# Adding the experts' rows to the residual stream by an accumulating scatter, in a one-core diffusion block with a mixture of experts

## The reference

```python
h2 = modulate(rmsnorm(x, g_norm2[i]), sh2, sc2)          # x * rstd * g * (1 + scale) + shift
moe = hierarchical_moe(h2, ...)                          # per token: best of 4 groups, best 2 of its 8 experts
#   gate  = top_w / sum(top_w) * p(group)                # one gate for each of a token's two experts
#   y     = (silu(x @ w_gate[e]) * (x @ w_up[e])) @ w_down[e]
#   moe   = zeros(n, d).at[slot_tok].add(y * slot_gate)  # each token gets two gated rows
x = x + gt2 * moe
return rmsnorm(x, g_final)
```

## Time and profile before

| | |
|---|---|
| runs, us | 1279.66, 1282.55, 1283.43; median 1282.55 |
| profiled execution, us | 1280.05, with a span of 1278.2 from first to last instruction |
| TensorE | busy 1225.1 us (96% of the span) |
| VectorE | busy 956.4 us (75%) |
| ScalarE | busy 679.8 us (53%) |
| GpSimd | busy 262.6 us (21%) |
| mean granted TensorE clock | 0.983 of full |
| moved by DMA | 344.34 MB, mean 269 GB/s |

### The profile page before, as it was taken

How to read it: one execution, slowest core, us unless ns; L and a number is a source line. 1 busy time by engine, 2 the same in 40 slices (tenths; PEclk the granted TensorE clock), 3 DMA queues, 4 the chain that set the end, 5 groups by cost and what they waited for, 6 DMA issues and landing times. The chain is left out here.

```text
span 1278.2 us, 18789 instructions
## 1 busy us (share of the span) xinstructions
PE 1225.1 (96%) x7362; PEld 1020.9 (80%) x7362; DVE 956.4 (75%) x1128; ACT 679.8 (53%) x806; POOL 262.6 (21%) x210
## 2 busy tenths in 40 slices
PE   5899999999999999999979999999999999999986
PEld 1799888888788888888768888888888888888863
DVE  2756554332678888666669999999999999999956
ACT  3832212111556666332247777777777777777722
POOL 0000000001100010000110634525355173611111
PEclk9899999999999999999899999999999999999988
DMA  9658844435576774610469999999999999999937
GB/s 380 244 187 294 285 148 155 159 113 171 201 227 143 186 176 109 216 58 34 143 232 370 369 399 384 383 389 374 387 380 382 385 369 398 382 387 374 379 121 303
DMA packets 95659, 344.34 MB, mean 269 GB/s; under 512 B 18459, under 2 KB 46803, under 8 KB 67923
## 3 DMA queue, kind: packets, MB, share of 16 engines
q1 hardware_dynamic: 74659, 311.89, 67.0%
q10 hardware_dynamic: 11696, 14.44, 3.9%
q0 software_dynamic: 9216, 16.80, 3.5%
HBM read 314.23 MB, written 39.34 MB: 277 GB/s over the span
## 5 line engine op out<-in xcount | busy, mean ns | idle before, releaser
L2150 DVE TENSOR_TENSOR w_low<-raw,w_high 128x2048 fp32r<-128x2048 f32 x130 | 296.1, 2298 | 6.2 <-ACT w_high L2096 6.1
L2096 ACT ACTIVATE w_high<-raw 128x2048 fp32r<-128x2048 f32 x130 | 244.5, 1908 | 8.5 <-PEq L1386 8.5
L2150 DVE TENSOR_TENSOR w_low<-arena,w_high 128x2048 fp32r<-128x2048 f32 x62 | 142.6, 2303 | 27.1 <-ACT w_high L2096 27.1
L2051 POOL DMA_INDIRECT y_rows<-arena,row x32 | 68.3, 2136 | 315.6 <-DVE arena L2172 314.1
L2096 ACT ACTIVATE w_high<-arena 128x2048 fp32r<-128x2048 f32 x62 | 118.2, 1907 | 0.0
L1996 PE MATMUL p_g<-w_high,x_high 128*128 128x512 f32 x252 | 102.3, 406 | 1.9 <-DVE w_low L2150 1.1
L1996 PE MATMUL p_u<-w_high,x_high 128*128 128x512 f32 x256 | 102.8, 402 | 0.0
L1996 PE MATMUL p_a<-tokens_high,half_high 128*128 128x512 f32 (+1 forms) x272 | 101.9, 374 | 0.2 <-DVE half_low L699 0.2
L1997 PE MATMUL p_a<-tokens_low,half_high 128*128 128x512 f32 (+1 forms) x272 | 101.0, 371 | 0.0
L1998 PE MATMUL p_a<-tokens_high,half_low 128*128 128x512 f32 (+1 forms) x272 | 100.9, 371 | 0.0
L1998 PE MATMUL p_u<-w_high,x_low 128*128 128x512 f32 x256 | 100.0, 391 | 0.0
(11 more groups left out here) (388 smaller groups left out, 2848.7 us busy)
## 6 DMA issues: line engine op xcount, KB each, us to landing
raw<-in_w_gate SPq DMA_DIRECT2D x64, 1024.0 KB, 8.4
raw<-in_w_up SPq DMA_DIRECT2D x64, 1024.0 KB, 8.5
arena<-in_w_down SPq DMA_DIRECT2D x62, 1024.0 KB, 8.5
raw<-in_w_ada SPq DMA_DIRECT2D x24, 1024.0 KB, 7.4
x<-qk_rows SPq DMA_DIRECT2D x6, 1664.0 KB, 8.7
raw<-in_w_chunks SPq DMA_DIRECT2D x9, 1024.0 KB, 5.6
qk_rows<-x SPq DMA_DIRECT2D x18, 512.0 KB, 2.6
mod<-x ACTq DMA_DIRECT2D x48, 128.0 KB, 3.3
```

The costliest lines, as they stand in the source:

```text
L2051: pool.indirect_dma_start(a.y_rows, bass.IndirectOffsetOnAxis(ap=s.row[:, n:n + 1], axis=0), x.y[b], None, bounds_check=2 * N - 1, oob_is_ ...
L2096: act.activation(x.high[i % SPLITS][:], x.raw[b][:, :], ACT.Copy).then_inc(high_ok, 1)
L2150: dve.tensor_tensor(x.low[i % SPLITS][:], x.raw[home(n, j)][:, :], x.high[i % SPLITS][:], ALU.subtract).then_inc(low_ok, 1)
```

## The change

1. **The stream is stored.** SP stores each tile of `s.x1` to a new DRAM array `stream_rows` (1024 rows) after `residual(n)`, between the weight loads that it issues there; `x_stored` counts them.
2. **The scatter accumulates.** It goes to `stream_rows` by `token`, with `compute_op=ALU.add`. Since a token's two rows now go to one place, each scatter first waits until the one before has landed. `y_rows` and `row` are gone.
3. **Gates by slot.** The gates are split into three bfloat16 parts, multiplied into the one-hot choice by VectorE at the head of the experts' block, and TensorE lists them by slot in 16 matmuls before the first expert. `move_y` multiplies by `slot_gates` in the same instruction. The table for tiles beyond 128 tokens gets gates in the same way: three GpSimd instructions and 16 matmuls more before expert 27.
4. **Only the sums are read back.** `finish` loads 512 KB for each tile into `s.x1`, squares, and scales. TensorE and GpSimd have no part in it; each group's Newton step is on VectorE.
5. **The last tile is modulated by VectorE**: one multiplication before `move_x(7)`, one fused multiply-add after its Newton step; the store waits for `scaled_last` 2.
6. `list_rows` is two instructions ahead of the gather, not four. `match` lives in the expert buffer `y5[0]`, so it waits for the store of tile 6.

```diff
-NORMS = [(0, 1), (1, 1), (2, 2), (4, 2), (6, 2)]
+NORMS = [(0, 1), (1, 2), (3, 2), (5, 2), (7, 1)]
@@ mix_and_route, SP
                 load_chunk(sp, a, s.raw[0], s.loaded[0], 0, 0)
+                def store_stream(i):
+                    sp.wait_ge(added, 2 * (i + 1))
+                    sp.dma_start(a.stream_rows[i * P:(i + 1) * P, :], s.x1[:, i, :]).then_inc(s.x_stored, 16)
+                for i in range(NT - 2):
+                    store_stream(i)
                 sp.wait_ge(split_low, 3 * NT - 2)
                 load_chunk(sp, a, s.raw[RING - 1], s.loaded[RING - 1], 0, RING - 1)
+                store_stream(NT - 2)
...
-                sp.wait_ge(scaled_last, 4)
+                sp.wait_ge(scaled_last, 1)
                 load_chunk(sp, a, s.raw[1], s.loaded[1], 0, 1)
                 sp.wait_ge(logits, NT + 1)
                 load_chunk(sp, a, s.raw[2], s.loaded[2], 0, 2)
+                store_stream(NT - 1)
@@ mix_and_route, GpSimd and ScalarE
-                pool.tensor_tensor(last[:], last[:], scale2, ALU.mult).then_inc(scaled_last, 1)
-                pool.tensor_tensor(last[:], last[:], shift2, ALU.add).then_inc(scaled_last, 1)
...
-                act.activation(xrow[(NT - 1) % 2][:], s.x1[:, NT - 1, :], ACT.Copy, scale=rstd[:, 2, NT - 1:NT])
@@ mix_and_route, VectorE
                     if n == NT - 1:
+                        dve.wait_ge(scaled_last, 1)
+                        stt(last[:], last[:], rstd[:, 2, one], shift2, ALU.mult, ALU.add).then_inc(scaled_last, 1)
+                def scale_last():
+                    dve.wait_ge(added, 2 * NT)
+                    dve.wait_ge(h_out[(NT - 1) % 2], 16 * (NT // 2 - 1))
+                    tt(xrow[(NT - 1) % 2][:], s.x1[:, NT - 1, :], scale2, ALU.mult).then_inc(scaled_last, 1)
...
+                dve.wait_ge(h_out[0], 16 * NT // 2)
...
+                for d in range(2):
+                    step(dve.tensor_copy(s.gate_parts[:, d, :], flat_gates))
+                    step(tt(flat_gates, flat_gates, s.gate_parts[:, d, :], ALU.subtract))
+                step(dve.tensor_copy(s.gate_parts[:, 2, :], flat_gates))
@@ main_experts, GpSimd
                 pool.wait_ge(y_ok, n + 1)
-                pool.indirect_dma_start(a.y_rows, ...s.row..., x.y[b], None, bounds_check=2 * N - 1).then_inc(scattered[b], 16)
+                pool.wait_ge(s.x_stored, 16 * NT) if n == 0 else pool.wait_ge(scattered, 16 * n)
+                pool.indirect_dma_start(a.stream_rows, ...s.token..., x.y[n % 2], None, bounds_check=N - 1,
+                                        compute_op=ALU.add).then_inc(scattered, 16)
@@ main_experts, VectorE
-                    dve.wait_ge(scattered[n % 2], 16 * (n // 2))
+                    dve.wait_ge(scattered, 16 * (n - 1))
-                dve.tensor_tensor(halves(x.y[n % 2]), p_y, halves(x.gate2[:]), ALU.mult)
+                dve.scalar_tensor_tensor(halves(x.y[n % 2]), p_y, s.slot_gates[:, n:n + 1], halves(x.gate2[:]), ALU.mult, ALU.mult)
+            def code_gates():                                   # called first in the block
+                for d in range(3):
+                    dve.tensor_tensor(x.gate_code[:, :, d, :], one_e, s.gate_parts[:, d, :]..., ALU.mult).then_inc(q.gate_coded, 1)
@@ main_experts, TensorE
+            def list_gates():                                   # called between stay_awake and turn_x(0)
+                pe.wait_ge(q.gate_coded, 3)
+                for u in range(2 * NT):
+                    listed = pe.matmul(x.p_list[:, 0:3 * NE], s.match[:, u, :], x.gate_code[:, u]...)
@@ finish
+        for i in range(NT):
+            sp.dma_start(s.x1[:, i, :], a.stream_rows[i * P:(i + 1) * P, :]).then_inc(x_in[i], 16)
...
+            for i in range(t0, t0 + n):
+                act.wait_ge(x_in[i], 16)
+                act.activation(junk[i], s.x1[:, i, :], ACT.Square, accum_out=ss[:, i:i + 1]).then_inc(rooted, 1)
+            act.activation(root[:, part], ss[:, part], ACT.Sqrt, ...).then_inc(rooted, 1)
...
+            c.step(dve.reciprocal(rstd[:, part], root[:, part]))
+            newton(dve, c, rstd[:, part], ss[:, part], tmp[:, part], D, n=1)
             for i in range(t0, t0 + n):
                 dve.scalar_tensor_tensor(x1, x1, rstd[:, i:i + 1], gains[:], ALU.mult, ALU.mult).then_inc(scaled, 1)
```

More of the change, by code:

```diff
@@ L1588, in norm_x @@
                     if n == NT - 1:
-                        dve.sem_inc(scaled_last, 1)
+                        last = xrow[n % 2]
+                        dve.wait_ge(scaled_last, 1)
+                        stt(last[:], last[:], rstd[:, 2, one], shift2, ALU.mult, ALU.add).then_inc(scaled_last, 1)
                         return
@@ L1686, in _ @@
                 dve.wait_ge(placed, 2)
-                list_rows(dve, c, p_t[0][:, 0:2 * NE], rowf[:], wrap[:], s.token[:], s.row[:], listed_ok)
+                list_rows(dve, c, p_t[0][:, 0:2 * NE], wrap[:], s.token[:], listed_ok)
                 step(dve.tensor_copy(total, p_r[:, NT * NE:(NT + 1) * NE]))
@@ L1808, in gather, with list_rows @@
                             bounds_check=N - 1, oob_is_err=False).then_inc(s.gathered[n % 2], 16)
-def list_rows(dve, c, digits, rowf, wrap, token, row, listed=None):
+def list_rows(dve, c, digits, wrap, token, listed=None):
     n = token.shape[1]
[L1815 to L1818, removed]
+    c.step(dve.tensor_scalar(wrap, digits[:, n:2 * n], float(N), None, ALU.add))
+    tokens = dve.scalar_tensor_tensor(token, digits[:, 0:n], -float(P), wrap, ALU.mult, ALU.add)
     if listed is None:
@@ L1849 @@
 class OverTables:
-    STEPS = 80
+    STEPS = 83
     def __init__(self, s, x):
@@ L2047, in scatter @@
             def scatter(n):
-                b = n % 2
                 pool.wait_ge(y_ok, n + 1)
-                pool.indirect_dma_start(a.y_rows, bass.IndirectOffsetOnAxis(ap=s.row[:, n:n + 1], axis=0), x.y[b], None,
-                                        bounds_check=2 * N - 1, oob_is_err=False).then_inc(scattered[b], 16)
+                if n == 0:
+                    pool.wait_ge(s.x_stored, 16 * NT)
+                else:
+                    pool.wait_ge(scattered, 16 * n)
+                pool.indirect_dma_start(a.stream_rows, bass.IndirectOffsetOnAxis(ap=s.token[:, n:n + 1], axis=0), x.y[n % 2], None,
+                                        bounds_check=N - 1, oob_is_err=False, compute_op=ALU.add).then_inc(scattered, 16)
             steps = Counter(pool, over_ready)
@@ L2074, in _ @@
                 if n == 16:
-                    over.blocks(pool, steps)
+                    over.blocks(pool, steps, s)
                 if n == 19:
@@ L2081, in _ @@
             count = spare.count(pool)
-            for b in range(2):
-                pool.wait_ge(scattered[b], 16 * (NE // 2))
+            pool.wait_ge(scattered, 16 * NE)
             spare.gpsimd(pool, count)
@@ L2168, in move_y, with add_parts @@
                 if n >= 2:
-                    dve.wait_ge(scattered[n % 2], 16 * (n // 2))
+                    dve.wait_ge(scattered, 16 * (n - 1))
                 halves = lambda y: y.rearrange("p (c n) -> p c n", c=2)
                 p_y = p_last if n == NE - 1 else x.p_y[:]
-                dve.tensor_tensor(halves(x.y[n % 2]), p_y, halves(x.gate2[:]), ALU.mult).then_inc(y_ok, 1)
+                dve.scalar_tensor_tensor(halves(x.y[n % 2]), p_y, s.slot_gates[:, n:n + 1], halves(x.gate2[:]), ALU.mult, ALU.mult).then_inc(y_ok, 1)
+            def code_gates():
+                one_e = over.one_e.rearrange("p (u e) -> p u e", e=NE)
+                for d in range(3):
+                    dve.tensor_tensor(x.gate_code[:, :, d, :], one_e, s.gate_parts[:, d, :].unsqueeze(2).to_broadcast([P, 2 * NT, NE]),
+                                      ALU.mult).then_inc(q.gate_coded, 1)
+            def add_parts(dst, parts):
+                c.step(dve.tensor_reduce(dst, parts.rearrange("p (d e) -> p e d", d=3), AX.X, ALU.add))
+            code_gates()
             split(0, 0)
@@ L2324, in _ @@
             spare.tensor(pe, spare.count(pe))
-            last.tensor(pe)
 def spare_blocks(t, a, s, x, q):
@@ L2517, in add @@
-        def add(i):
-            n = summed.index(i)
-            dve.wait_ge(gathered, n + 1)
-            dve.tensor_tensor(halves(s.x1[:, i, :]), halves(s.x1[:, i, :]), p_s[n % 2], ALU.add).then_inc(added, 1)
-        def invert(g):
-            t0, n = NORMS[g]
+        for g, (t0, n) in enumerate(NORMS):
             part = slice(t0, t0 + n)
             dve.wait_ge(rooted, 1 + t0 + n + g + 1)
-            dve.reciprocal(rstd[:, part], root[:, part]).then_inc(inverted, 1)
-        def scale(g):
-            t0, n = NORMS[g]
-            part = slice(t0, t0 + n)
-            if g < len(NORMS) - 1:
-                dve.wait_ge(refined, 1 + 5 * (g + 1))
-            else:
-                dve.wait_ge(inverted, g + 1)
-                newton(dve, c, rstd[:, part], ss[:, part], tmp[:, part], D, n=1)
+            if g == 0:
```

(3 more changed lines are left out.)

163 lines of the change are left out of this document (50 added, 113 removed).

## The result

The changed kernel takes 1293.76 us in the median (1292.54 to 1301.54, six runs); the kernel before, run beside it, takes 1284.13 (1279.66 to 1286.19). The ratio is 1.0086, with a 95% interval of 1.0066 to 1.0106, which makes about 11 us; the two medians are 9.6 apart. The change is slower, where 1265 was forecast. The profiled execution took 1293.67 us, its span is 1291.5.

What follows compares the result with a forecast made beforehand. In the expert loop TensorE and the DMA engines both looked full, with TensorE ending last. Terms -16.2 - 3.2 + 0.7 + 0.45 + 2.0 = -16.25 on 1280.05 gave 1263.8, stated as 1265; range 1260 to 1286.

Steps and rivals of the forecast that it cites:

- The finish: From first read-back to end: 24.6 us instead of 40.8, VectorE becoming the limit; -16.2 us.
- The choice and the way in: Choice of experts: two VectorE instructions no longer wait for GpSimd, -3.2 us; 16 gate matmuls before the first expert, +0.7.
- SP's queue and the barrier: Stream stores queued ahead of weight loads, and the barrier before the experts: both taken as 0 us.
- The last scatters: End of the experts: accumulating scatter lands in 4.6 us, last one starts 0.6 late; +2.0 with the gate, bounds 0 to 5.7.
- The loop: Expert loop: waits between scatters hidden and DMA engines have room for the added reads; 0 us, bounds 0 and +20.
- The second rival: Expert loop: DMA engines full and one more read paid, 0.7 us x 29 = +20, total 1284 us; chance 0.12.
- The third and fourth rivals: Expert loop: accumulating row costs three plain ones, 1305 us (chance 0.14); scatters become a chain, 1329 us (chance 0.04).

Runs made afterwards that it cites:

- run 10: The kernel before with only the last tile modulated by VectorE (part 5 of the change); 1277.81 us, ratio 0.9965.
- run 1: The changed kernel with a plain scatter in place of the accumulating one, all else kept; 1265.23 us, ratio 0.9873.
- run 11: The kernel before with the last tile modulated by VectorE and finish tiles 5 and 7 summed wholly by TensorE; 1278.94 us, ratio 0.9966.
- runs 4 and 7 to 9: Changed kernel with half the scatters accumulating (1269.93 us); ten weight buffers (1282.61); ten buffers and shorter GpSimd table pieces (1282.05); shorter pieces alone (1295.71).
- run 5's first form: The changed kernel with weight loads of experts 2 to 31 bringing only 112 of 128 partitions; 1485.58 us.
- run 9: The changed kernel, six weight buffers, with only GpSimd's table worked out in shorter pieces; 1295.71 us, ratio 1.0115.
- run 3: The kernel before with each scatter issued a second time, plain, to another array; 1307.56 us, ratio 1.0200.

## Why the prediction was wrong, point by point

- **The finish** (-16.2): right. -16.0 measured. After the first group VectorE waits only once, ahead of the second, as worked out group by group (1.14 us, 0.3 forecast), and ends 21.7 us after the first issue (21.5 forecast).
- **The choice and the way in** (-3.2 + 0.7): the mechanism was right, the size is less sure. The ranks come right behind the 54 transposes in every run with this part. But the first `p_x` is earlier by 2.7 us in run 10, 2.3 in run 1, 1.2 in the changed kernel and 0.2 in run 11, which has the same program as run 10 up to there. Two things differ from execution to execution: when the stretch begins (VectorE's `residual` of the last tile, at 623.56 before, is at 624.69 in run 10 and 625.55 in run 11), and the clock of the 24 transposes behind the list. In the changed kernel they take 4.48 us at a granted clock of 0.62, for 2.82 at 1.00 in the earlier trace rows; they take 2.82 in runs 1 and 10 too, and 4.48 in run 11. `list_gates` takes 0.84 (0.7 forecast). The changed kernel's line (timeline):

```profile
644.38 4.48 PE L288 MATMUL p_y<-ident 128*128 128x128 f32 x24
```

- **SP's queue and the barrier** (0): nothing to see in run 1, which has them.
- **The last scatters** (+2.0, bounds 0 to 5.7): mis-sized. I took 4.6 us for a landing; it is 6.0 to 6.2. And I had the last one start 0.6 late: it starts 3.8 us after its rows are ready (DVE 1255.30 + 1.28, issue 1260.43), for 0.8 before, since the two ahead of it follow one another. That is 3.1 + 2.7; +6.3 was measured in all, just beyond the bound.
- **The loop** (0, bounds 0 to +20): the step that failed. It read: "The share of 1.00 says there is no room; the 400 GB/s over 20 us in the same loop and 414 elsewhere say there is the earlier trace rows, and chunks may land up to 3.5 us later than now. I take 0". Three things were wrong in it. The 400 is one window of 20 us, little more than one expert; over 140 and 150 us of the kernel before it was 384 and 379, at a share of 1.00. The slack in landing (3.5 us in that row, about 10 in all by runs 4 and 7 to 9) is a stock, used up once by a drain of about 1.1 us for each expert, not a discount on each of 29. And waiting costs more than its length, because the clock falls behind it (4.0 us lost by the wait of 2.2). The second rival ("DMA engines are full and one more read is paid", 0.12) was the right mechanism, with +20 for +24; the time came out at its 1284 plus the end's 4 more and the loop's 4 more. That its +20 came so near is partly luck: it took 0.7 us for each expert where the drain is 1.1, and no reserve where there was one of 10 us, and the two errors nearly cancel. The third and fourth rivals are refuted: a row costs as much as two plain ones, not three, and scatters land in 11.9 us in the median of the loop (9.9 before), far from 17.77.

## What to carry to other kernels

- When two resources are full in a loop, price what a change adds on each of them separately, and take the mean over many periods as the capacity, never the best short window. A slack in landing time is a stock: divide it by the drain of each period and see whether it lasts to the end.
- An accumulating scatter took twice the engine time of a plain one here. What it saved was a read-back of 4.2 MB, with a finish 16 us shorter; what it cost was 24 us in a loop with full engines. Run 1, with the same finish and without that cost, took 18.5 us less than the kernel before.
- In a loop that is bound by the total work of a resource, the wait that the profile names may be only the place where the loss is taken. Remove it and see whether the length changes, before calling it a cause.

## What the runs showed of the hardware that was not expected

- Loading 112 of 128 partitions is slower than loading all. In run 5's first form `q1` carried 32.95 MB in 87.5% of 150 us, 251 GB/s of engine time, for 52.51 MB in 90.7%, 386 GB/s, in run 1. The edit changes nothing but which partitions a load covers; why that is slower wasn't tried.
- Beside accumulating rows the packets of the weights' queue `q1` take a little longer: 384 GB/s of its engine time before (52.92 MB in 91.8% of 150 us), 379 after (50.24 MB in 88.3%), 376 in run 9 (50.19 MB in 89.1%). With doubled plain rows it is 378 (50.30 MB in 88.6%).
- GpSimd's instruction for an accumulating scatter takes 2.66 us in the mean, for 2.14 in the kernel before. Its gathers take 2.08 for 1.45, but that isn't particular to accumulating: beside doubled plain scatters (run 3) they take 2.01, and beside single plain ones (run 1) 1.48.
